# The dense stages of a decoder step in one block: the next stage begins on tiles 0 to 2 while tiles 3 and 4 are normalised

## The chip, the cores and the metric

The kernel runs on one core of a Trainium2 chip. The metric is the device time of one execution in microseconds (us); smaller is better. The core has five engines with a queue of their own: TensorE (PE), VectorE (DVE), ScalarE (ACT), GpSimd (POOL) and SyncE (SP), which here issues the loads. They meet through semaphores, and at the end of a block in a barrier of all engines.

## The reference

One step of a decoder of two layers, for 528 prompt tokens (16 of them learned) and 64 new tokens of 8 sequences, that is 592 tokens of width 1024. All is float32.

```
for l in range(DEPTH):                                    # DEPTH = 2, alpha = (2 * DEPTH) ** 0.25
    x = layernorm(alpha * x + 0.5 * swiglu(x, ffn1_w_in[l], ffn1_w_out[l]), ln1)
    z = x @ w_in[l]                                       # queries, keys, values, indexer, latents
    o = sparse_attention(z, cache_dsa) | latent_attention(z, cache_mla)
    x = layernorm(alpha * x + o @ w_o[l], ln2)
    x = layernorm(alpha * x + 0.5 * swiglu(x, ffn2_w_in[l], ffn2_w_out[l]), ln3)

def swiglu(x, w_in, w_out):                               # inner width 2816
    g, u = split(x @ w_in)
    return (silu(g) * u) @ w_out
```

## The kernel before

The 592 tokens are five tiles of rows: four of 128 and one of 80 (tile 4). `T.x` holds the residual, tokens on partitions. `T.xth` and `T.xtl` hold its transpose in two parts, a rounded high part and the remainder, so that a product in three passes (high x high, high x low, low x high) keeps float32's accuracy. Weights come in blocks of 128 x 1024 (512 KB) through a ring: SP loads one into one of four `raw` buffers, ACT rounds it into `whi` (`hi`, line 128), DVE subtracts into `wlo` (`lo`, line 132), both with two buffers, and PE uses it; `w_used` counts finished weights and frees the buffers.

The layer loop is a loop on the device (`Fori`). Its body is a row of blocks; each begins with branches and ends with a barrier that clears the block's semaphores: feed-forward 1 (`ffn_block`), projection (`proj_block`), index, prompt attention, two sample blocks, output projection (`mix_out_block`), feed-forward 2.

A feed-forward block first computes 44 products of width 592 (two matmuls of 296 columns for each of 8 slices and three passes, line 467, 48 per weight; the weight is the stationary operand); ACT takes silu, DVE multiplies, POOL splits the result into `hth` and `htl`. Then `out_stage` multiplies by the second weight, with the tokens stationary, in two groups: tiles 0 to 2 over all 22 slices, then tiles 3 and 4 (lines 140 to 142, 512 columns). While the second group runs, tiles 0 to 2 are normalised and transposed. `mix_out_block` uses the same `out_stage` with 8 slices and no first product.

The normalisation of a tile is a chain: DVE adds the product to alpha times x (`ln_sum`, 194) and takes the statistics (201, 203), ACT the root (211), DVE the reciprocal and the shift (217, 219), POOL scales and shifts, multiplies by the gain and adds the bias (227, 231, 233). For tiles 3 and 4 DVE does 640 of the 1024 columns (240, 244) and POOL the rest. Then PE transposes (260), ACT copies the high part (269), DVE subtracts the low part (274). For tiles 3 and 4 all this comes behind the last matmul, and the next block's first load is issued behind the barrier.

The projection multiplies by 14 weight parts: four column chunks of 338 in three slices of the inner dimension (`z_part`), and two parts of 384 columns for the latent queries (`q_part`). `Z_BANK` and `Q_BANK` say which PSUM bank each tile's result takes; small transposes (`job`) stand between the last parts, beginning with that of `wuk`. Every engine's order is that in which the code is written.

Of the kernel before, what the change touches and what calls it, by code (L numbers as in the profile page):

```python
# [88 lines left out]

class Map:  # L90
# [19 lines left out]
def stream_ops(T, S):  # L110
# [13 lines left out]
    def hi(e, n, s, round_, width=BLK, first=False):  # L124
        e.wait_ge(raw_in[s], round_ * 16 + 16)
        if not first:
            e.wait_ge(S.w_used, n - (SPLIT - 1))
        e.activation(T.whi[:, s % SPLIT, 0:width], T.raw[:, s, 0:width], ACT.Copy).then_inc(S.hi_done, 1)  # L128

    def lo(e, n, s, width=BLK):  # L130
        e.wait_ge(S.hi_done, n + 1)
        e.tensor_tensor(T.wlo[:, s % SPLIT, 0:width], T.raw[:, s, 0:width],  # L132
                        T.whi[:, s % SPLIT, 0:width].bitcast(F32), ALU.subtract).then_inc(S.split_done, 1)
# [14 lines left out]
TPB = {0: 2, 1: 4, 2: 2, 3: 4, 4: 2}  # L148


def out_stage(nc, T, S, kt, n0, lhs_hi, lhs_lo, scale, first_wait):
# [14 lines left out]
    rest = [t for t in GROUPS[0] if t not in turn.values()]  # L166

    def sp(e, weight, ln_g, ln_b, l):
        for g in range(2):
            for k in range(kt):  # L170
                n = n0 + g * kt + k
                load(e, n, n % RAW, weight(k), first=n < RAW)
                if g == 0 and k == kt // 2:
                    ln_wait = T.gb_free(S)
                    if ln_wait:
                        e.wait_ge(*ln_wait)
                    for i, a in enumerate((ln_g, ln_b)):
                        e.dma_start(T.gb[:, i, :], a[bass.ds(l, 1), :].partition_broadcast(P)).then_inc(S.gb_in, 16)
# [43 lines left out]
    def ln_d(e, t):  # L222
# [3 lines left out]
        e.wait_ge(S.nb_done, t + 1)  # L226
        e.tensor_scalar(x, x, T.rstd[0:r, t:t + 1], T.nb[0:r, t:t + 1], ALU.mult, ALU.add).then_inc(S.norm_done, 1)  # L227
# [5 lines left out]
        e.tensor_tensor(x, x, T.gb[0:r, 1, c], ALU.add).then_inc(S.x_done, 1)  # L233

# [12 lines left out]
    def ln_e(e, t):  # L247
# [5 lines left out]
        if t < 2:  # L253
            e.wait_ge(S.evac_done, 2 * (t + 1) + 2)
        else:
            e.wait_ge(S.xtl_done, t - 1)
        for k in range(KD):
            if t >= 3 and k == NV // P:
                e.wait_ge(S.x_done, t + 1)
            mm = e.transpose(T.ps[:, TPB[t] + k // 4, (k % 4) * P:(k % 4) * P + r],  # L260
# [3 lines left out]
    def tp(t):  # L264
        return T.ps[:, TPB[t]:TPB[t] + 2, :].rearrange("p b (q c) -> p (b q) c", q=4)[:, :, 0:ROWS[t]]
# [10 lines left out]
    def act(e):  # L276
        for g in range(2):
            for k in range(kt):
                n = n0 + g * kt + k + 2
                if n < n0 + 2 * kt:  # L280
                    act_split(e, n)
                if g == 1 and k in std_at:
                    ln_b(e, std_at[k])
                if g == 1 and k in turn:
# [4 lines left out]
        ln_b(e, 4)  # L289
        ln_f(e, 3)  # L290
        ln_f(e, 4)

    def dve(e):
        for g in range(2):
            for k in range(kt):
# [3 lines left out]
                if n < n0 + 2 * kt:  # L299
                    lo(e, n, n % RAW)  # L300
                if g == 1 and k > 0 and k in sum_at:
# [10 lines left out]
        for t in rest:  # L312
            ln_g(e, t)
        ln_dv(e, 3)
        ln_c(e, 4)
        ln_dv(e, 4)
# [7 lines left out]
    def pe(e):  # L324
# [24 lines left out]
        for t in [*rest, 3, 4]:  # L349
            ln_e(e, t)  # L350

    return sp, act, dve, pool, pe


FFN_SEMS = LN_SEMS + STREAM_SEMS + ["silu_done", "hmul_done", "hhi_done", "hlo_done"]


def ffn_block(nc, T, S, l, w_in, w_out, ln_g, ln_b):
# [4 lines left out]
    N1 = 2 * KF  # L363

# [5 lines left out]
    T.gb_free = lambda S_: (S_.hlo_done, KF)  # L370
    sp2, act2, dve2, pool2, pe2 = out_stage(nc, T, S, KF, N1, T.hth, T.htl, 0.5, first_wait)
# [4 lines left out]
    with nc.Block() as block:  # L376
        @block.sync
        def _(e):
            def four(i, first):
                for u in range(4):  # L380
                    j = 2 * i + u // 2
                    col = (u % 2) * D_FF + j * P
                    src = w_in[bass.ds(l, 1), :, bass.ds(col, P)].rearrange("l (k p) c -> p (l k) c", p=P)
                    load(e, 4 * i + u, u, src, shape=(KD, P), first=first)
            four(0, True)
            with e.Fori(1, KF // 2) as i:
                four(i, False)
            sp2(e, lambda k: w_out[bass.ds(l, 1), k * P:(k + 1) * P, :].rearrange("l p n -> p (l n)"), ln_g, ln_b, l)

        @block.scalar  # L390
        def _(e):
            def silu(i, u, first=False):
                e.wait_ge(S.w_used, 4 * i + 2 * u + 2)
                if not (first and u == 0):
                    e.wait_ge(S.hmul_done, 2 * i + u)
                e.activation(T.silu[:, :].rearrange("p (h c) -> p h c", h=2), bank(u, 0), ACT.Silu).then_inc(S.silu_done, 1)

            def body(i, first):
                for u in range(2):
# [2102 lines left out]
```

## Time and profile before

| | us |
|---|---|
| median of three runs | 3438.72 (3434.47 to 3439.16) |
| the profiled execution | 3437.44 |
| its span, first to last instruction | 3435.7 |
| PE busy | 3001.9 (87%) |
| weight loads of PE (beside it) | 2573.6 (75%) |
| DVE busy | 1428.0 (42%) |
| ACT busy | 999.6 (29%) |
| POOL busy | 624.9 (18%) |

The mean clock granted to TensorE was 0.933 of full speed. Busy times of matmuls overlap, since the next starts before the last has drained: the pace is the distance from start to start. A wait is shown with the engine, line and result that ended it. Names in the rows are those of the program, without buffer numbers.

### The profile page before, as it was taken

To read this page: it belongs to the slowest core of one execution; us is meant where nothing else is said; L and a number is where in the kernel's file an instruction comes from. 1 tells how busy PE (TensorE), PEld (TensorE's weight loads), DVE (VectorE), ACT (ScalarE), POOL (GpSimd) and SP (SyncE) were. 2 spreads that over 40 slices of the span, in tenths; PEclk is the share of its full clock that TensorE was granted. 3 is DMA by queue.
4 is the path that set the end of the run, shared out by engine and by line. 5 is a ranking of instruction groups with operands and counts; after the bars stand their busy time and mean duration, and the time that the engine had idled before them with its cause. 6 is when DMAs were issued, how large, how long until landed. Compare 5 with 4: busy or idle time off the path is not lost. (4 is left out here: it accounts for less than half of the span.)

```text
span 3435.7 us, 46122 instructions
## 1 busy us (share of the span) xinstructions
PE 3001.9 (87%) x18298; PEld 2573.6 (75%) x18298; DVE 1428.0 (42%) x2110; ACT 999.6 (29%) x1602; POOL 624.9 (18%) x568
## 2 busy tenths in 40 slices
PE   6999979768797879999889999796787978799997
PEld 6999759545565669998689997684555656699985
DVE  2222363466764352222622224434676643422236
ACT  2212233434342221212321223234344422212223
POOL 1111030213122131110311111211121121311103
PEclk9999989879898989999989999898798989899998
DMA  3222431300122322224432234313001223222244
GB/s 111 81 81 86 142 126 51 123 1 1 62 79 77 121 76 80 79 80 134 123 93 79 80 109 141 102 39 123 1 1 62 94 90 113 68 80 81 82 140 126
DMA packets 241752, 293.93 MB, mean 86 GB/s; under 512 B 12624, under 2 KB 205488, under 8 KB 235456
## 3 DMA queue, kind: packets, MB, share of 16 engines
q1 hardware_dynamic: 234688, 229.00, 22.2%
q0 software_dynamic: 6912, 62.92, 5.0%
q8 instruction: 94, 1.54, 0.2%
q14 instruction: 58, 0.48, 0.0%
HBM read 287.72 MB, written 3.88 MB: 85 GB/s over the span
## 5 line engine op out<-in xcount | busy, mean ns | idle before, releaser
L132 DVE TENSOR_TENSOR wlo<-raw,whi 128x1024 fp32r<-128x1024 f32 (+2 forms) x412 | 537.0, 1304 | 1430.5 <-ACT whi L128 1429.2
L128 ACT ACTIVATE whi<-raw 128x1024 fp32r<-128x1024 f32 (+2 forms) x412 | 433.5, 1052 | 1564.8 <-PE ps L467 928.4
L467 PE MATMUL ps<-xth,whi 128*128 128x296 f32 x2816 | 810.7, 300 | 42.3 <-DVE wlo L132 42.3
L467 PE MATMUL ps<-xtl,whi 128*128 128x296 f32 x2816 | 812.8, 301 | 0.0
L467 PE MATMUL ps<-xth,wlo 128*128 128x296 f32 x2816 | 615.6, 300 | 0.0
L467 PEld LDWEIGHTS ps<-xth,whi 128*128 128x128 f32 x2816 | 533.7, 190 | 43.2 <-DVE wlo L132 43.2
L467 PEld LDWEIGHTS ps<-xtl,whi 128*128 128x128 f32 x2816 | 532.2, 189 | 0.0
L467 PEld LDWEIGHTS ps<-xth,wlo 128*128 128x128 f32 x2816 | 460.7, 189 | 0.0
L140 PE MATMUL ps<-whi,hth 128*128 128x512 f32 (+1 forms) x880 | 350.7, 398 | 9.9 <-DVE wlo L132 8.3
L142 PE MATMUL ps<-whi,htl 128*128 128x512 f32 (+1 forms) x880 | 346.9, 394 | 0.0
L141 PE MATMUL ps<-wlo,hth 128*128 128x512 f32 (+1 forms) x880 | 346.8, 394 | 0.0
L446 POOL CAST hth<-hf 128x592 f32 x88 | 59.7, 678 | 989.0 <-DVE hf L417 989.0
L140 PE MATMUL ps<-whi,xth 128*128 128x338 f32 (+1 forms) x480 | 175.2, 365 | 43.4 <-DVE wlo L132 43.0
L140 PEld LDWEIGHTS ps<-whi,hth 128*128 128x128 f32 (+1 forms) x880 | 158.5, 180 | 67.7 <-DVE wlo L132 21.7
L142 PEld LDWEIGHTS ps<-whi,htl 128*128 128x128 f32 (+1 forms) x880 | 158.2, 180 | 45.9
L141 PEld LDWEIGHTS ps<-wlo,hth 128*128 128x128 f32 (+1 forms) x880 | 158.4, 180 | 42.1
L141 PE MATMUL ps<-wlo,xth 128*128 128x338 f32 (+1 forms) x480 | 170.0, 354 | 0.0
L142 PE MATMUL ps<-whi,xtl 128*128 128x338 f32 (+1 forms) x480 | 169.4, 353 | 0.0
L227 POOL TENSOR_SCALAR x<-x,rstd,nb 128x1024 f32<-128x1024 f32 (+2 forms) x30 | 34.7, 1158 | 652.7 <-DVE nb L219 652.7
L1599 ACT ACTIVATE pP<-ps,pnmx 128x256 f32<-128x256 f32 (+4 forms) x132 | 70.3, 532 | 232.9 <-DVE pnmx L1676 232.5
L140 PEld LDWEIGHTS ps<-whi,xth 128*128 128x128 f32 x480 | 91.5, 191 | 55.4 <-DVE wlo L132 46.1
L448 POOL TENSOR_TENSOR htl<-hf,hth 128x592 f32 x88 | 129.0, 1466 | 14.4 <-POOL hth L446 14.4
(378 smaller groups left out, 4014.8 us busy)
## 6 DMA issues: line engine op xcount, KB each, us to landing
raw<-in_ffn_w_in SPq DMA_DIRECT2D x176, 512.0 KB, 3.8
raw<-in_ffn_w_out SPq DMA_DIRECT2D x176, 512.0 KB, 3.5
raw<-in_w_o SPq DMA_DIRECT2D x32, 512.0 KB, 3.6
raw<-in_w_in SPq DMA_DIRECT2D x16, 507.0 KB, 3.7
gb<-in_ln_g SPq DMA_DIRECT2D x6, 512.0 KB, 4.6
gb<-in_ln_b SPq DMA_DIRECT2D x6, 512.0 KB, 6.0
raw<-in_w_in SPq DMA_DIRECT2D x8, 338.0 KB, 3.4
x<-in_x_prompt SPq DMA_DIRECT2D x1, 1536.0 KB, 10.8
```

The source lines that it names most:

```text
L128: e.activation(T.whi[:, s % SPLIT, 0:width], T.raw[:, s, 0:width], ACT.Copy).then_inc(S.hi_done, 1)
L132: e.tensor_tensor(T.wlo[:, s % SPLIT, 0:width], T.raw[:, s, 0:width], T.whi[:, s % SPLIT, 0:width].bitcast(F32), ALU.subtract).then_inc(S. ...
L140: e.matmul(out, lhi, rhi, start=start, stop=False)
L141: e.matmul(out, lhi, rlo, start=False, stop=False)
L142: return e.matmul(out, llo, rhi, start=False, stop=stop)
L227: e.tensor_scalar(x, x, T.rstd[0:r, t:t + 1], T.nb[0:r, t:t + 1], ALU.mult, ALU.add).then_inc(S.norm_done, 1)
L446: e.tensor_copy(h_hi, T.hf[:, u, :]).then_inc(S.hhi_done, 1)
L448: e.tensor_tensor(h_lo, T.hf[:, u, :], h_hi.bitcast(F32), ALU.subtract).then_inc(S.hlo_done, 1)
L467: mm = e.matmul(bank(u, up)[:, h, :], part[:, s, w], xp[:, k, o], start=(k == 0 and part is T.whi and xp is T.xth), stop=(k == KD - 1 and ...
L1599: e.activation(Pb[:, i % 3, 0:NK[t]], SB(p["s"], P, NK[t]), ACT.Exp, bias=nmx[:, i % 3:i % 3 + 1], accum_out=rsum[:, a, c:c + 1]).then_inc ...
```

## The change

The blocks of a run of dense stages become one block: feed-forward 1 and projection of layer 0; then output projection, feed-forward 2, feed-forward 1 of the next layer and its projection; at the end output projection and feed-forward 2. Five barriers with their semaphore clears fall away. The layer loop is written out in Python, since the last run of stages differs. Semaphores of the weight ring count on through a block (offset `B`), each stage has its own set for the rest.

- Weights of the next stage are loaded and split in the tail of the one before (`nxt.hi`, `nxt.lo`): two in the last two steps of the second group, two more between the steps of tiles 3 and 4. Up to four go to new buffers `awhi`, `awlo`, which lie over rows 0 to 13 of `hth`.
- A feed-forward stage that has one before it begins with four pieces on tiles 0 to 2 (384 columns), with the transposes of tiles 3 and 4 between them, and then four pieces on tiles 3 and 4 (208 columns). Its silu and product for these weights are made in two parts.
- The projection begins with its first six weight parts on tiles 0 to 2, the two transposes between, and then does the six on tiles 3 and 4.
- In the output projection the scale and shift of tiles 0 to 2 move from POOL to ACT (`ln_n`).
- Tile 3 and 4 are transposed into banks 6, 7 and 0, 1 (before a projection both into 0, 1); `Z_BANK`, `Q_BANK` and what the jobs wait for follow.
- Loads of the projection's gains, `wuk` and `wuv` are issued behind the load of its sixth part and behind the end of the normalisation. POOL scales x by alpha tile by tile behind the transposes.

```diff
@@ out_stage
+    act_norm = kt <= 12
@@ transposes, ln_e
-        else:
-            e.wait_ge(S.xtl_done, t - 1)
+        elif t == 2:
+            e.wait_ge(S.xtl_done, 1)
+        elif t == 3:
+            e.wait_ge(S.evac_done, 10 if tpb[0] == 0 else 8)
+        else:
+            e.wait_ge(S.evac_done, 10)
+            e.wait_ge(S.xtl_done, 4 if tpb[0] == tpb[1] else 1)
@@ ACT of out_stage
                 if n < n0 + 2 * kt:
                     act_split(e, n)
+                elif nxt:
+                    nxt.hi(e, n - n0 - 2 * kt)
                 if g == 1 and k in std_at:
                     ln_b(e, std_at[k])
+                if g == 1 and act_norm and k - 1 in std_at:
+                    ln_n(e, std_at[k - 1])
...
         ln_b(e, 4)
+        if nxt:
+            nxt.hi(e, 2)
+            nxt.hi(e, 3)
         ln_f(e, 3)
         ln_f(e, 4)
@@ DVE of out_stage
         for t in rest:
             ln_g(e, t)
+        if nxt:
+            nxt.lo(e, 2)
         ln_dv(e, 3)
         ln_c(e, 4)
+        if nxt:
+            nxt.lo(e, 3)
         ln_dv(e, 4)
@@ PE of a feed-forward stage
+        if early:
+            e.wait_ge(S0_.xtl_done, 3)
+            for u in range(2):
+                for up in range(2):
+                    cols, out = early_parts(u, up)[0]
+                    piece(2 * u + up, cols, out).then_inc(S.early_ps, 1)
+                    if up == 1 - u:
+                        stage.turn(e, 3 + u)
+            e.wait_ge(S0_.xtl_done, 5)
+            for u, up in ((1, 0), (0, 0), (0, 1), (1, 1)):
+                cols, out = early_parts(u, up)[1]
+                piece(2 * u + up, cols, out).then_inc(S.w_used, 1)
+        else:
             body(0, True)
@@ projection
-Z_BANK = [(0, 1, 2, 3, 4), (5, 6, 7, 0, 1), (2, 3, 4, 0, 1), (7, 3, 4, 5, 6)]
-Q_BANK = [(5, 6, 7, 2, 3), (4, 0, 1, 5, 6)]
+Z_BANK = [(2, 3, 4, 0, 1), (5, 6, 7, 2, 3), (4, 0, 1, 2, 3), (7, 4, 2, 3, 5)]
+Q_BANK = [(5, 6, 7, 4, 0), (1, 2, 3, 5, 6)]
...
                 elif b == 0:
-                    q_gone(e, 1, 1)
-                    q_gone(e, 1, 2)
+                    q_gone(e, 0, 4)
+                    q_gone(e, 1, 0)
...
-            for n in range(8):
-                z_part(n)
+            e.wait_ge(S0_.xtl_done, 3)
+            for n in range(3):
+                z_part(n, (0, 1, 2))
+            ln_e(e, 3)
+            e.wait_ge(S0_.evac_done, 8)
+            z_part(3, (0, 1, 2))
+            ln_e(e, 4)
+            z_part(4, (0, 1, 2))
+            z_part(5, (0, 1, 2))
+            e.wait_ge(S0_.xtl_done, 5)
+            for n in range(6):
+                z_part(n, (3, 4))
+            z_part(6)
+            z_part(7)
@@ build
-        with nc.Fori(0, DEPTH) as l:
-            ffn_block(nc, T, ffn_s, l, W["ffn1_w_in"], W["ffn1_w_out"], W["ln1_g"], W["ln1_b"])
-            proj_block(nc, T, proj_s, l, W, O)
+        dense_block(nc, T, dense_s, W, O, None, 0)
+        for l in range(DEPTH):
             index_block(nc, T, index_s, l, W["cache_dsa"])
             prompt_block(nc, T, prompt_s)
             sample_block(nc, T, sample_s, l, "M", W["cache_mla"], O["mla_s"], W["cache_dsa"])
             sample_block(nc, T, sample_s, l, "D", W["cache_dsa"], O["dsa_s"])
-            mix_out_block(nc, T, ffn_s, l, W["w_o"], W["ln2_g"], W["ln2_b"])
-            ffn_block(nc, T, ffn_s, l, W["ffn2_w_in"], W["ffn2_w_out"], W["ln3_g"], W["ln3_b"])
+            dense_block(nc, T, dense_s, W, O, l, l + 1 if l + 1 < DEPTH else None)
```

TensorE, from the output projection into feed-forward 2, before: the last matmuls on tile 4, the transposes of tiles 2 to 4 (`ident`, `x`), the branches of block end and begin, the first product.

```order
L142 MATMUL ps<-whi_53,xtl_51 80x512
L260 MATMUL ps<-ident_58,x_49 128x128 x16
L260 MATMUL ps<-ident_58,x_49 128x80 x8
L2417 UNCONDITIONAL_BRANCH
L451 UNCONDITIONAL_BRANCH
L467 MATMUL ps<-xth_50,whi_53 128x296
```

TensorE at the same place now (`awhi` and `awlo` are the weights split ahead):

```order
L168 MATMUL ps<-whi_53,xtl_51 80x512
L300 MATMUL ps<-ident_58,x_49 128x128 x8
L580 MATMUL ps<-xth_50,awhi_83 128x384
...
L580 MATMUL ps<-xth_50,awlo_84 128x384
L300 MATMUL ps<-ident_58,x_49 128x128 x8
L580 MATMUL ps<-xth_50,whi_53 128x384
...
L580 MATMUL ps<-xth_50,wlo_54 128x384
L300 MATMUL ps<-ident_58,x_49 128x80 x8
L580 MATMUL ps<-xth_50,whi_53 128x384
...
L580 MATMUL ps<-xth_50,wlo_54 128x384
L580 MATMUL ps<-xth_50,whi_53 128x208
```

The transposes of tile 3 stand behind 48 matmuls of 384 columns, those of tile 4 behind 24 more, and the width of 208 follows behind 24 more again.

VectorE, at the end of feed-forward 1 and the beginning of the projection, before:

```order
L203 BN_AGGR mv<-stats 80x2
L240 SCALAR_TENSOR_TENSOR x<-x,mv,gb 128x640
L244 SCALAR_TENSOR_TENSOR x<-x,rstd,gb 128x640
L217 RECIPROCAL rstd<-std 80x1
...
L244 SCALAR_TENSOR_TENSOR x<-x,rstd,gb 80x640
L274 TENSOR_TENSOR xtl<-ps,xth 128x8x128
L274 TENSOR_TENSOR xtl<-ps,xth 128x8x80
L376 UNCONDITIONAL_BRANCH
L997 UNCONDITIONAL_BRANCH
L1055 MEMSET z 64x1352
L1056 MEMSET qpe 64x256
L132 TENSOR_TENSOR wlo<-raw,whi 128x1014 x2
```

VectorE at the same place now:

```order
L232 BN_AGGR mv<-stats 80x2
L159 TENSOR_TENSOR awlo<-raw,awhi 128x676
L275 SCALAR_TENSOR_TENSOR x<-x,mv,gb 128x640
L279 SCALAR_TENSOR_TENSOR x<-x,rstd,gb 128x640
L246 RECIPROCAL rstd<-std 80x1
L248 SCALAR_TENSOR_TENSOR nb<-mv,rstd 80x1
L159 TENSOR_TENSOR awlo<-raw,awhi 128x1014
L275 SCALAR_TENSOR_TENSOR x<-x,mv,gb 80x640
L279 SCALAR_TENSOR_TENSOR x<-x,rstd,gb 80x640
L314 TENSOR_TENSOR xtl<-ps,xth 128x8x128
L314 TENSOR_TENSOR xtl<-ps,xth 128x8x80
L1228 MEMSET z 64x1352
```

A weight split (`awlo`) stands ahead of each of tiles 3's and 4's normalised columns; the memsets of `z` and `qpe` still stand behind the last subtraction, in front of the fifth weight's split.

ScalarE at the same place before, from the last weight copy of the feed-forward stage:

```order
L128 ACTIVATE whi<-raw 128x1024
L211 ACTIVATE std<-mv,eps 128x1
L211 ACTIVATE std<-mv,eps 80x1
L269 ACTIVATE xth<-ps 128x8x128
L269 ACTIVATE xth<-ps 128x8x80
L376 UNCONDITIONAL_BRANCH
L929 UNCONDITIONAL_BRANCH
L128 ACTIVATE whi<-raw 128x1014 x2
L128 ACTIVATE whi<-raw 128x676
```

ScalarE now:

```order
L153 ACTIVATE whi<-raw 128x1024
L153 ACTIVATE awhi<-raw 128x1014 x2
L240 ACTIVATE std<-mv,eps 128x1
L240 ACTIVATE std<-mv,eps 80x1
L153 ACTIVATE awhi<-raw 128x676
L153 ACTIVATE awhi<-raw 128x1014
L309 ACTIVATE xth<-ps 128x8x128
L309 ACTIVATE xth<-ps 128x8x80
L153 ACTIVATE whi<-raw 128x1014
L153 ACTIVATE whi<-raw 128x676
```

Four weight copies have moved ahead of the copies of tiles 3 and 4 (`xth`); the fifth, of the second slice of chunk 1, stands behind both.

## Rows read from the trace of the kernel before

**Rows 1.** Page, parts 1 and 2: busy time, slices of TensorE.
```profile
PE 3001.9 (87%) x18298; PEld 2573.6 (75%) x18298; DVE 1428.0 (42%) x2110; ACT 999.6 (29%) x1602; POOL 624.9 (18%) x568
...
PE   6999979768797879999889999796787978799997
```

**Rows 2.** Waits of PE, whole span: us in total, times, longest us.
```profile
PE ps L140 <- DVE wlo L132: 54.8, 18, 13.6
...
PE ps L467 <- DVE wlo L132: 42.3, 4, 12.4
```

**Rows 3.** Stretches: us, busy of PE PEld DVE ACT POOL, PEclk, DMA, GB/s.
```profile
484.40:508.60 24.20, 3.56 (x16) 2.68 (x16) 12.94 (x21) 4.26 (x6) 7.65 (x9) 0.56 0.31 100
1708.80:1732.80 24.00, 3.56 (x16) 2.68 (x16) 11.53 (x19) 4.65 (x6) 11.52 (x11) 0.58 0.23 63
1236.30:1257.00 20.70, 3.56 (x16) 2.68 (x16) 11.76 (x19) 5.11 (x7) 11.53 (x11) 0.63 0.28 74
```

**Rows 4.** Timeline, feed-forward to projection, layer 0: start, us, engine, line [idle <-releaser].
```profile
483.99 0.40 PE L142 MATMUL ps<-whi,htl 128*80 128x512 f32 x1
...
490.19 0.89 DVE L244 SCALAR_TENSOR_TENSOR x<-x,rstd,gb 128x640 f32<-128x640 f32 x1
...
492.23 1.10 DVE L244 SCALAR_TENSOR_TENSOR x<-x,rstd,gb 80x640 f32<-80x640 f32 x1
...
494.27 0.99 POOL L233 TENSOR_TENSOR x<-x,gb 80x384 f32<-80x384 f32 x1
...
501.76 8.77 SPq L122 DMA_DIRECT2D raw<-in_w_in  x6
...
506.27 1.05 ACT L128 ACTIVATE whi<-raw 128x1014 fp32r<-128x1014 f32 x1 [9.55 <-DMA raw<-in_w_in]
...
508.62 0.65 PE L140 MATMUL ps<-whi,xth 128*128 128x338 f32 x1 [12.64 <-DVE wlo L132]
```

**Rows 5.** Chain that ended last, in order of time: start, us, what.
```profile
2960.18 291.81 PE ps L467 x2112
...
3378.57 0.87 PE ps L260 x8
```

**Rows 6.** Timeline of PE, first latent product: first and last of 24 intervals.
```profile
571.00 0.33 PE L141 MATMUL ps<-wlo,cqh 128*128 128x384 f32 x1
...
575.19 0.33 PE L141 MATMUL ps<-wlo,cqh 128*80 128x384 f32 x1
```

**Rows 7.** Stretches of PE: us, PE busy (instructions), PEclk, DMA share, GB/s.
```profile
508.60:515.00 6.40, 6.38 (x24) 0.53 0.60 171
518.60:525.60 7.00, 7.00 (x47) 1.00 0.28 74
1226.40:1229.40 3.00, 2.95 (x11) 0.50 0.00 0
1272.70:1708.80 436.10, 433.64 (x2701) 1.00 0.33 100
```

**Rows 8.** Timeline of ACT: the weight copies that end the compared stretches.
```profile
548.92 1.05 ACT L128 ACTIVATE whi<-raw 128x1014 fp32r<-128x1014 f32 x1 [3.59 <-PE ps L142]
...
1285.95 1.06 ACT L128 ACTIVATE whi<-raw 128x1024 fp32r<-128x1024 f32 x1 [5.51 <-PE ps L467]
...
1761.13 1.06 ACT L128 ACTIVATE whi<-raw 128x1024 fp32r<-128x1024 f32 x1 [5.51 <-PE ps L467]
```

**Rows 9.** Timeline: two waits of PE, two instructions of DVE.
```profile
586.59 1.11 PE L1163 MATMUL ps<-ident,wuk 128*128 128x128 f32 x4 [3.87 <-DVE qpe L1053]
...
1215.81 3.24 DVE L132 TENSOR_TENSOR wlo<-raw,whi 128x1024 fp32r<-128x1024 f32 x1
...
1226.45 1.97 PE L260 MATMUL ps<-ident,x 128*128 128x128 f32 x8 [4.30 <-POOL x L233]
...
1240.04 1.17 DVE L274 TENSOR_TENSOR xtl<-ps,xth 128x1024 fp32r<-128x1024 f32 x1
```

**Rows 10.** Page, part 5: the weight splits; busy us, mean ns | idle.
```profile
L132 DVE TENSOR_TENSOR wlo<-raw,whi 128x1024 fp32r<-128x1024 f32 (+2 forms) x412 | 537.0, 1304 | 1430.5 <-ACT whi L128 1429.2
```

More of the change, by code:

```diff
@@ new lines, in weight_lo, with sync, four @@
+    def weight_lo(e, n):
+        lo(e, B + n, n % RAW, ahead=AHEAD.get(n))
+    stage.nxt = Ahead(weight_hi, weight_lo)
+    def sync(e):
+        def four(i, first):
+            for u in range(4):
+                j = 2 * i + u // 2
+                col = (u % 2) * D_FF + j * P
+                src = w_in[bass.ds(l, 1), :, bass.ds(col, P)].rearrange("l (k p) c -> p (l k) c", p=P)
+                load(e, B + 4 * i + u, u, src, shape=(KD, P), first=first)
+        four(0, B == 0)
+        with e.Fori(1, KF // 2) as i:
+            four(i, False)
+        stage.sp2(e, lambda k: w_out[bass.ds(l, 1), k * P:(k + 1) * P, :].rearrange("l p n -> p (l n)"), ln_g, ln_b, l)
@@ new lines, in tensor, with piece, body @@
+    def tensor(e):
+        def piece(n, cols, out):
+            w_hi = T.awhi[:, AHEAD[n], :] if n in AHEAD else T.whi[:, n % SPLIT, :]
+            w_lo = T.awlo[:, AHEAD[n], :] if n in AHEAD else T.wlo[:, n % SPLIT, :]
+            e.wait_ge(S.split_done, B + n + 1)
+            for k in range(KD):
+                w = slice(k * P, (k + 1) * P)
+                for part, xs in ((w_hi, (T.xth, T.xtl)), (w_lo, (T.xth,))):
+                    for xp in xs:
+                        mm = e.matmul(out, part[:, w], xp[:, k, cols], start=(k == 0 and part is w_hi and xp is T.xth),
+                                      stop=(k == KD - 1 and part is w_lo))
+            return mm
+        def body(i, first):
+            for u in range(2):
+                for up in range(2):
+                    n = 4 * i + 2 * u + up
+                    s = up % SPLIT
+                    e.wait_ge(S.split_done, B + n + 1)
+                    if up == 0 and not first:
+                        e.wait_ge(S.hmul_done, 2 * i + u - 1)
+                    for k in range(KD):
+                        w = slice(k * P, (k + 1) * P)
+                        for part, xs in ((T.whi, (T.xth, T.xtl)), (T.wlo, (T.xth,))):
+                            for h in range(2):
+                                o = slice(h * HALF, (h + 1) * HALF)
+                                for xp in xs:
+                                    mm = e.matmul(bank(u, up)[:, h, :], part[:, s, w], xp[:, k, o],
+                                                  start=(k == 0 and part is T.whi and xp is T.xth),
+                                                  stop=(k == KD - 1 and part is T.wlo))
+                    mm.then_inc(S.w_used, 1)
+        if early:
+            e.wait_ge(S0_.xtl_done, 3)
+            for u in range(2):
+                for up in range(2):
+                    cols, out = early_parts(u, up)[0]
[6 more added lines that the diff above has]
+                piece(2 * u + up, cols, out).then_inc(S.w_used, 1)
+        else:
+            body(0, True)
+        with e.Fori(1, KF // 2) as i:
+            body(i, False)
+        stage.pe2(e)
+        if stage.last:
+            stage.ln_e(e, 3)
+            stage.ln_e(e, 4)
@@ L478, with begin, end @@
+    def begin(ln_e):
+        stage.turn = ln_e
+    def end(nxt, tpb=(6, 0)):
+        stage.sp2, stage.act2, stage.dve2, stage.pool2, stage.pe2, stage.ln_e = \
+            out_stage(nc, T, S, KF, B + N1, T.hth, T.htl, 0.5, first_wait, nxt, tpb, gb_free=(S.hlo_done, KF))
+        stage.last = nxt is None
+    stage.begin, stage.end = begin, end
+    stage.parts = (sync, scalar, vector, gpsimd, tensor)
+    return stage
 C_ROPE = 0
```

449 lines of the change are left out of this document (264 added, 185 removed).

## The prediction

> **What bounds the kernel now.** The page's first part has TensorE busy 87% of the span and every other engine under half [rows 1]: time is won where TensorE stands still or is slow. The waits of TensorE say where. Its two costliest kinds of wait on a weight split (`wlo`, line 132) are few and long: 54.8 us in 18 waits, the longest 13.6, and 42.3 us in only 4 [rows 2]. Waits that long sit at the stage boundaries. The table of stretches shows three kinds of them: 24.2 us behind the first feed-forward stage, 24.0 between the two layers, 20.7 behind an output projection, each with 3.6 us of TensorE work, the transposes [rows 3]. The five that the change touches (two of the first kind, one, two) are some 114 us, 3.3% of the span.
>
> The order of time in the first one [rows 4]: the last matmul ends at 484.4; VectorE finishes tile 3's normalised columns at 491.1 and tile 4's at 493.3, GpSimd tile 4's at 495.3; then the barrier; only at 501.8 is the first weight load issued, ScalarE splits it at 506.3, TensorE starts at 508.6. And it starts slowly: for 6.4 us the granted clock is 0.53, the lower level, about 3 us lost [rows 7].
>
> **Pace of TensorE.** 296 columns: 291.81 us for 2112 matmuls, 0.138 us each, 0.137 without the slow start. 384 columns: 24 matmuls in 4.19 us (571.00 to 575.19), 0.175. 338 columns: 7.00 us for a chunk's 45, 0.156. Eight transposes of 128 columns: 0.87, 0.109 each [rows 5 to 7]. The change makes a width that the trace lacks, 208 columns: not under the transposes' 0.109, not over 0.137 of the 296 columns; the line through 296 and 384 would give 0.10. I take 0.11, near the lower row. The four early weights then cost 96 x (0.175 + 0.11) = 27.4 us instead of 192 x 0.137 = 26.3: 1.1 us more per stage, up to 3.7.
>
> The Trainium skill, TensorE: Matmul & The Clock Gate, section LDWEIGHTS, gives a 128-column weight load 128/1.2 = 107 ns, which would be a floor for the narrow pieces. The transposes' 109 ns agrees, so by the rule too they cost 0.11.
>
> **Between the layers (one boundary).** Counted from the end of the last matmul, t = 0. The first two weights are split ahead, into space that the second product has left, while its last steps run: ScalarE and VectorE are mostly idle there. Pieces (0,0) and (0,1) on 384 columns end at 8.4. The transposes of tile 3 want its normalised columns. Before, these were there at 6.7 (491.1 less 484.4). Now the split of weight 2 stands ahead of them on VectorE: it waits for ScalarE, which copies only behind tile 4's root (some 1.4), and takes 1.3 itself (mean 1304 ns) [rows 4, 10]; 0.4 more come from the splits ahead of tile 3's sums. So 9.7, a wait of 1.3. Then 0.9 transposes, 4.2 piece, tile 4 (ready at about 14.1: 10.9 before, plus a second split and the delay, less what GpSimd does beside it; reached at 14.8), 0.8, 4.2, and four narrow pieces 10.6: 30.4 us for four weights. Before, ScalarE took the sixth weight at 1761.1, when TensorE had done with four: 52.3 us after 1708.8 [rows 3, 8]. Gain 21.9. What runs beside it on ScalarE (silu in two parts) and on GpSimd (the scaling by alpha, tile by tile behind the transposes) has 6.6 us of matmuls per weight to hide in.
>
> **Feed-forward to projection (two).** Three weights on tiles 0 to 2: 72 x 0.156 = 11.2; transposes 0.9; fourth weight 4.2; transposes of tile 4 0.7: t = 17.0. The next weight is not ready. Its copy stands on ScalarE behind the copy of tile 4 (0.7), and on VectorE the subtraction of tile 4 (0.8), two memsets (1.5) and the split (1.2) come one after another: 21.4, so 4.4 us idle. Then 45 + 96 matmuls, 22.0, and 0.8 for weight 6, whose buffer comes free only 12 matmuls before it is wanted: 44.2. An idle time of this length is answered by the lower clock: behind 4.30 us of idle the three microseconds from 1226.4 ran at 0.50, 1.5 lost, and a little more behind them [rows 7, 9]. I put 2 us: 46.2. Before, the same point was at 548.9, 64.5 us after the last matmul [rows 8]. Gain 18.3 each, 36.6.
>
> **Output projection to feed-forward (two).** Here tile 2 is transposed last, and its low part is subtracted on VectorE behind the sums of tiles 3 and 4: at 1240.04 for 1.17 [rows 9]. The first early piece waits for it: TensorE stands still from 1236.3 to about 1240.7, and pays 2 us of lower clock. Then 8.4 + 0.9 + 4.2 + 0.8 + 4.2 + 10.6 = 29.1: 1271.8, against 1285.9 before [rows 8]. Gain 14.1 each, 28.3. Inside this stage the first affine step of tiles 0 to 2 moves from GpSimd to ScalarE. Tile 0 gets later by about 0.5 us (it stands behind a weight copy), tile 1 earlier by about 1, so the 4.30 us wait at 1226.45 shrinks a little; tile 2 stands behind the copy of tile 1's transposes and a weight copy. I take nothing; it can be 3 either way.
>
> **Inside the projection (two).** New PSUM banks: the transposes of `wuk` waited 3.87 us for a `qpe` copy of VectorE [rows 9]; now they want only copies that ScalarE makes first, and the VectorE copy is wanted by tile 2, one tile later. Some 1 us of wait stays; with the clock 3.5 us each, 7.0 (bounds 0 and 11).
>
> **Things costed at nothing.** The layer loop is written out. Code entered for the first time shows no cost: TensorE's slices read alike, within a tenth or two, in the loop's first pass (the first 20) and its second [rows 1]. The parameter loads move behind the weights of the projection and behind the end of the normalisation, about 30 us before they are wanted.
>
> **Sum.** 21.9 + 36.6 + 28.3 + 7.0 = 93.8. The profiled execution took 3437.4 (span 3435.7), 1.3 under the median: 3438.7 - 94 = 3344.7. I predict 3344.
>
> A rule that speaks against it: the Trainium skill, GPSIMD Engine Reference, Specifications, says that GpSimd shares its SBUF interfaces with VectorE, and that instructions of VectorE with two SBUF inputs contend. The weight split is one, and the change puts two of them into the tail where GpSimd normalises. The trace agrees that a split can take 3.24 us [rows 9]. By the rule the tail is up to 3.9 us longer per boundary; this is the first rival.
>
> **Rivals.**
> 1. The tail grows. Splits beside GpSimd take 3.24 instead of 1.30 us [rows 9, 10]: two per boundary, 3.9 us, five times: 19 us, and some more half clock, about 3368. For it: tile 4's work on GpSimd falls beside the second split. Against: between the sums and that, GpSimd has finished tile 3, and TensorE has 8 to 17 us of pieces in hand.
> 2. Narrow matmuls are slow. If one of 208 columns costs as two passes of 0.11, 288 of them cost 32 us more: 3376. Nothing in the trace has that width; the 8 transposes at 0.109 speak against it.
> 3. The waits that I see are shorter and the clock stays up: five waits of 4 us with 2 us each would give back up to 18: 3326.
> 4. The pieces start no earlier: their weights wait for rows of the second product or for raw buffers. Only the barrier and the load (12 us per boundary) would be saved at most, perhaps half: about 3400.
> 5. Slower. Without its pauses TensorE is granted the lower clock for long. The place is the feed-forward stage behind each boundary, 292 us of its first product. A quarter of that work at half speed adds 73 us, three times 219: 3563. It decides from 188 us at half clock, whose half eats the gain. Against: 1272.7 to 1708.8 ran without a pause at 1.00 [rows 7]; every fall follows idle time.
>
> **How the numbers follow.** The forecast 0.62, rival 1 0.17, rival 2 0.06, rival 3 0.09, rival 4 0.03, rival 5 0.03. The range: downwards rival 3 (3326). Upwards the bounds together: narrow pieces at 0.137 (+8), tail 2 us longer each (+10), nothing from the banks (+7), clock 3 instead of 2 (+4): 3373; to take in rival 2, 3376. About 0.9 would lie inside by the cases; I leave it, since several of these terms are unseen. A change under 0.2% (7 us) could not be told from none: faster 0.96, within 0.01, slower 0.03.
>
> **What would show it.** TensorE's waits on `wlo` fall from about 100 to about 45 us. Between the layers TensorE has no gap over 2 us. Behind each feed-forward stage there is one gap of 4 to 5 us in front of the fifth projection weight, behind each output projection one of about 4.5 in front of the first 384-column matmul. The 208-column matmuls start 0.11 us apart. The granted clock dips below 1 only behind those gaps; its mean rises from 0.933 to about 0.94. It is wrong if a gap over 6 us stays at any of the five, or if the half clock lasts over 5 us behind one.

## The result and the profile after

The changed kernel takes 3344.0 us (median of 4 runs, 3343.0 to 3345.8), the kernel before 3438.1 on the same chip: a ratio of 0.9729, 95% interval 0.9712 to 0.9746. The forecast was 3344. The profiled execution took 3345.84 us, with a span of 3343.8 against 3435.7, and a mean granted clock of 0.946 against 0.933.

Page, part 1 and TensorE's slices, as in [rows 1]:

```profile
PE 2992.7 (90%) x18298; PEld 2567.1 (77%) x18298; DVE 1424.6 (43%) x2116; ACT 1002.0 (30%) x1612; POOL 623.7 (19%) x562
...
PE   6999998768797889999999999986888968899997
```

TensorE is busy for 9 us less than before, in a span 92 us shorter. The dips of the slices to 7 at the stage boundaries are gone, but for an 8 at the end of each output projection; what is left is attention. The waits of PE (us in total, times, longest us); L166 was L140, L598 was L467, L159 was L132 [rows 2]:

```profile
PE ps L166 <- DVE wlo L159: 37.9, 20, 8.4
...
PE ps L300 <- POOL x L263: 16.9, 7, 3.6
...
PE ps L598 <- DVE wlo L159: 11.9, 1, 11.9
...
PE ps L580 <- DVE xtl L314: 6.5, 2, 3.6
...
PE ps L166 <- DVE qpe L1225: 1.9, 2, 0.9
```

97.1 us on weight splits have become 49.8, and 11.9 of these are the kernel's first weight, which nothing can precede. Stretches of the kernel after (us, busy of PE PEld DVE ACT POOL, PEclk, DMA share, GB/s), to be held against [rows 3, 7, 8]:

```profile
484.77:506.60 21.83, 17.14 (x117) 16.90 (x115) 15.41 (x26) 5.51 (x8) 8.72 (x9) 1.00 0.32 106
506.60:510.20 3.60, 3.60 (x13) 3.60 (x14) 0.72 (x1) 0.00 (x0) 0.00 (x0) 0.53 0.97 309
510.20:531.20 21.00, 20.33 (x130) 19.41 (x128) 1.63 (x3) 2.18 (x4) 0.00 (x0) 1.00 0.02 6
1145.43:1249.94 104.51, 92.78 (x472) 78.33 (x473) 53.03 (x66) 32.81 (x37) 30.90 (x20) 0.94 0.38 121
1672.80:1703.12 30.32, 29.28 (x209) 28.91 (x208) 14.84 (x24) 7.29 (x10) 13.84 (x13) 1.00 0.31 89
```

The fourth row is the first output projection up to the fourth early weight. The last row is the boundary between the layers: four weights in 30.3 us, TensorE busy for 29.3 of them, full clock. Behind a feed-forward stage (first three rows) the one pause ends at 506.60, and the clock is 0.53, the lower of its two levels, for 3.6 us behind it. The timeline shows what that pause is made of:

```profile
502.68 0.82 DVE L314 TENSOR_TENSOR xtl<-ps,xth 128x640 fp32r<-128x640 f32 x1 [3.19 <-ACT xth L309]
503.84 1.19 DVE L1228 MEMSET z<- 64x1352 f32 x1 [0.34 <-issue]
505.03 0.27 DVE L1229 MEMSET qpe<- 64x256 f32 x1
505.33 1.99 DVE L159 TENSOR_TENSOR wlo<-raw,whi 128x1014 fp32r<-128x1014 f32 x2
...
506.60 0.61 PE L166 MATMUL ps<-whi,xth 128*128 128x338 f32 x1 [4.69 <-DVE wlo L159]
```

VectorE is idle for 3.19 us, then has tile 4, two memsets and the split in a row. ScalarE's copy of that weight ended at 503.6, before the memsets began. The same in the other projection (4.70).

**Where the 92 us are.** Each stretch is taken between the same points of both traces: it begins with the end of the feed-forward stage's last matmul or with the start of the output projection's first one, and ends where ScalarE begins the weight copy that waits for the last of these weights, as in [rows 8] (up to 0.3 us behind the end of the matmuls, where the rows above end).

| stretch | before | after | gain | forecast |
|---|---|---|---|---|
| end of feed-forward to six projection weights done, layer 0 / 1 | 64.5 / 65.2 | 46.1 / 46.5 | 18.4 / 18.7 | 18.3 / 18.3 |
| first output projection to four weights done | 118.9 | 104.8 | 14.2 | 14.1 |
| second output projection, the same | 119.2 | 106.3 | 12.8 | 14.1 |
| between the layers, four weights | 52.3 | 30.4 | 21.9 | 21.9 |
| projection, latent product to attention, layer 0 / 1 | 56.8 / 58.2 | 53.8 / 53.9 | 2.9 / 4.4 | 3.5 / 3.5 |

The sum is 93.3, the spans differ by 91.9; the rest of the program is 1.4 us longer (the first stage by 1.4, the attention stages -1.9 and +1.8, which is less than their scatter, see layers_written_out). In the five boundary stretches, 86.1 us shorter, TensorE's busy time fell from 310.7 to 299.6 us: 75 us are time that it no longer stands still, 11 are matmuls that no longer run at the lower clock.

### The profile page after: what moved, and what is told of

It is laid out like the page before. It is cut to its first block and busy times, and to the rows that moved or that the text cites. A ratio compares the mean times of both kernels' runs of the same rounds, so it can differ in the third digit from the quotient of the medians.

```text
span 3343.8 us, 45553 instructions
## 1 busy us (share of the span) xinstructions
PE 2992.7 (90%) x18298; PEld 2567.1 (77%) x18298; DVE 1424.6 (43%) x2116; ACT 1002.0 (30%) x1612; POOL 623.7 (19%) x562
## 5 line engine op out<-in xcount | busy, mean ns | idle before, releaser
L159 DVE TENSOR_TENSOR wlo<-raw,whi 128x1024 fp32r<-128x1024 f32 (+2 forms) x398 | 512.0, 1288 | 1295.3 <-ACT whi L153 1294.2
L598 PE MATMUL ps<-xth,whi 128*128 128x296 f32 x2624 | 752.7, 299 | 11.9 <-DVE wlo L159 11.9
L598 PE MATMUL ps<-xtl,whi 128*128 128x296 f32 x2624 | 755.2, 300 | 0.0
L598 PE MATMUL ps<-xth,wlo 128*128 128x296 f32 x2624 | 572.3, 300 | 0.0
L598 PEld LDWEIGHTS ps<-xth,whi 128*128 128x128 f32 x2624 | 495.2, 189 | 12.0 <-DVE wlo L159 12.0
L598 PEld LDWEIGHTS ps<-xtl,whi 128*128 128x128 f32 x2624 | 493.9, 188 | 0.0
L598 PEld LDWEIGHTS ps<-xth,wlo 128*128 128x128 f32 x2624 | 428.0, 189 | 0.0
L166 PE MATMUL ps<-whi,hth 128*128 128x512 f32 (+1 forms) x880 | 350.6, 398 | 10.0 <-DVE wlo L159 8.3
L166 PEld LDWEIGHTS ps<-whi,hth 128*128 128x128 f32 (+1 forms) x880 | 158.5, 180 | 67.8 <-DVE wlo L159 22.5
L166 PE MATMUL ps<-whi,xth 128*128 128x338 f32 (+3 forms) x370 | 137.3, 371 | 28.3 <-DVE wlo L159 26.2
L167 PE MATMUL ps<-wlo,xth 128*128 128x338 f32 (+3 forms) x370 | 132.7, 359 | 0.0
L168 PE MATMUL ps<-whi,xtl 128*128 128x338 f32 (+3 forms) x370 | 132.3, 358 | 0.0
L1724 PE MATMUL ps<-z,pPT 128*128 128x128 f32 (+1 forms) x672 | 105.1, 292 | 22.6 <-DVE posb L1888 22.6
## 6 DMA issues: line engine op xcount, KB each, us to landing
x<-in_x_prompt SPq DMA_DIRECT2D x1, 1536.0 KB, 10.4
```

The costliest lines, as they stand in the source:

```text
L159: e.tensor_tensor(w_lo, T.raw[:, s, 0:width], w_hi.bitcast(F32), ALU.subtract).then_inc(S.split_done, 1)
L166: e.matmul(out, lhi, rhi, start=start, stop=False)
L167: e.matmul(out, lhi, rlo, start=False, stop=False)
L168: return e.matmul(out, llo, rhi, start=False, stop=stop)
L598: mm = e.matmul(bank(u, up)[:, h, :], part[:, s, w], xp[:, k, o], start=(k == 0 and part is T.whi and xp is T.xth), stop=(k == KD - 1 and ...
L1724: mm = e.matmul(flat[:, o:o + w], PT[0:kr, u % 2, k * P:(k + 1) * P], v, start=k == kts[0][0], stop=k == kts[-1][0])
```

## The experiments

Each was timed in five rounds (no_overlap in three) beside the kernel before, in three batches, each on another chip. The changed kernel was not timed again with them, so variants of it are compared with it by their ratios to the kernel before; a ratio of 0.001 is 3.4 us, and two such ratios are each known to about 0.0015.

### banks_alone

```
-Z_BANK = [(0,1,2,3,4), (5,6,7,0,1), (2,3,4,0,1), (7,3,4,5,6)]
-Q_BANK = [(5,6,7,2,3), (4,0,1,5,6)]
+Z_BANK = [(2,3,4,0,1), (5,6,7,2,3), (4,0,1,2,3), (7,4,2,3,5)]
+Q_BANK = [(5,6,7,4,0), (1,2,3,5,6)]     # and their waits
```

> The kernel before with nothing changed but the PSUM banks of the projection and the waits that follow from them. The theory of the prediction: 3.5 us less in each of two projections, so 3438.1 - 7 = 3431 us; in the profile the 3.87 us wait of the wuk transposes for a qpe copy shrinks to about 1 us. Rival: the copies of the other engine are as late, and the wait only changes its name and place: 3438 us, the sum of TensorE's waits inside the projection unchanged.

3431.8 us, ratio 0.9979 (0.9970 to 0.9989): 7.2 us less. The wait of [rows 9] is gone from the `wuk` transposes and one of 0.94 stands a tile later; timeline of PE in banks_alone:

```profile
588.15 0.42 PE L140 MATMUL ps<-whi,xth 128*128 128x338 f32 x1 [0.94 <-DVE qpe L1053]
```

From the latent product to attention it is 53.5 us instead of 56.8. The rival (the wait only changes its name) is out.

### no_overlap

```
 e.wait_ge(S0_.xtl_done, 3)
+stage.turn(e, 3); stage.turn(e, 4)      # transposes of tiles 3 and 4
+e.wait_ge(S0_.xtl_done, 5)
 ... pieces, without transposes between; the projection alike
```

> The changed kernel with TensorE's order put back at all five boundaries: tiles 3 and 4 are transposed and split first, and only then come the first weights' matmuls, on all tiles. One block, no barrier, and the weights loaded and split ahead as in the changed kernel. By my reasons the overlap is worth 13 us between the layers (four weights done 44 us after the last matmul, not 30.4), 10 at each of the two boundaries to the projection and 6 at each of the two behind an output projection: 45 us, and with five pauses of 10 to 16 us some 3 us more, so 3344 + 48 = 3392 us. If the barrier and the weight load were the whole gain: 3344 to 3350. If the overlap were all of it: about 3430.

3406.2 us, ratio 0.9907 (0.9891 to 0.9922): of the 94 us only 32 are left, so the overlap of the tail with matmuls is worth 62, two thirds. Of the 32 some 7 belong to the new PSUM banks (banks_alone), which this kernel has too. What is left for the barriers that are gone, the weights that are loaded and split early, the loop written out and the shifted affine step is about 25 us by the times, 30 by the traces of the five boundaries (420.1 to 389.8 us), a quarter to a third. No run takes these apart. TensorE's timeline in no_overlap, behind the first feed-forward stage and between the layers:

```profile
492.72 1.94 PE L300 MATMUL ps<-ident,x 128*128 128x128 f32 x8 [8.87 <-DVE x L279]
497.13 1.36 PE L300 MATMUL ps<-ident,x 80*128 80x80 f32 x8 [2.47 <-DVE xtl L314]
500.14 0.65 PE L166 MATMUL ps<-awhi,xth 128*128 128x338 f32 x1 [1.65 <-DVE xtl L314]
...
1705.01 1.94 PE L300 MATMUL ps<-ident,x 128*128 128x128 f32 x8 [9.53 <-DVE x L279]
```

And the stretch that answers to the 30.3 us:

```profile
1695.32:1741.46 46.14, 32.72 (x210) 31.71 (x209) 14.81 (x24) 7.28 (x10) 13.72 (x13) 0.82 0.20 58
```

The last piece ends 46.1 us after the last matmul, forecast 44: the pauses are answered by a mean clock of 0.82, where the changed kernel has 1.00 at this boundary. Over the five boundaries the traces show 56 us lost (389.8 instead of 334.1), forecast 48. TensorE's busy time there is 313.1 instead of 299.6 us, so the lower clock took 13.5 us, where I had put 3; standing still took 42, where I had put 45. The timed runs lost 62; 6 of these I cannot place. The profiled execution (span 3398) was the fastest of the four.

### layers_written_out and banks_and_written_out

```
-        with nc.Fori(0, DEPTH) as l:
+        for l in range(DEPTH):
```

> The kernel before with the loop over the layers written out, no other edit. The prediction costed this at nothing: 3438 us, within 2. Rival: code entered for the first time has to be fetched and the second layer is slower by more than it was: some 5 to 20 us longer, with gaps of all engines at the stage starts of the second layer. Other rival: constant addresses in place of registers shorten the start of every stage: 3430 us.

3432.5 us, ratio 0.9977 (0.9968 to 0.9986): 7.9 us less for an edit that I had costed at nothing. The second rival came near in the time (3430), but not in its mechanism: the start of the projection of layer 0 is no shorter (13.70 us of wait for its first weight, 12.64 before). To see whether that stands, the loop was written out on top of banks_alone:

> The kernel before with the new PSUM banks of the projection and with the layer loop written out. The two together, if layers_written_out measured something that stands: 3438.5 x 0.9979 x 0.9977 = 3423 us. If its 8 us were chance: 3431 us, as banks_alone. In the profile I look at the stretch between the layers, where the first weight's wait was 12.43 us with the loop and 9.84 without: about 9.8 again if it belongs to the loop's end, 12.3 to 13.7 as at the other boundaries if not.

3423.0 us, ratio 0.9945 (0.9932 to 0.9959): it stands. The first feed-forward matmul of the second layer, at 1732.81 behind 12.43 us of wait in the kernel before, in layers_written_out and in banks_and_written_out:

```profile
1734.19 0.61 PE L467 MATMUL ps<-xth,whi 128*128 128x296 f32 x1 [9.84 <-DVE wlo L132]
```

```profile
1727.13 0.62 PE L467 MATMUL ps<-xth,whi 128*128 128x296 f32 x1 [9.12 <-DVE wlo L132]
```

So the loop's end costs 2.6 us (12.43 to 9.84) to 4.6 (13.70 in banks_alone to 9.12). The wait for the first projection weight of layer 1 is 12.33 us in both, instead of 13.62 and 13.01, but the same wait in layer 0, which the edit does not touch, lies anywhere between 12.64 and 13.70 in these four traces, so that difference shows nothing. The other 3 to 5 of the 8 us stay open. The attention stages, where they could be, scatter too much to tell: that of layer 0 takes 537.5 to 545.8 us in kernels that have the same code for it. In the changed kernel the 2.6 to 4.6 us are part of the waits that the overlap removes, and so cannot be had twice.

### no_scalar_affine

```
-    act_norm = kt <= 12
+    act_norm = False
```

> The changed kernel with the affine step of tiles 0 to 2 of the output projection back on GpSimd. The prediction costed this edit at nothing, with 3 us per stage either way. Having seen the profile after, I expect 3345 us, within 2: the transposes of tile 2 may start a microsecond earlier or later, but the first early piece waits for VectorE, which takes tile 2's low part only behind the sums of tiles 3 and 4 (1217.32). Rival: GpSimd is the bound of the stage, and one more pass over three tiles (1.2 to 2.1 us each) shows at full price: 3344 + 2 x 4 = 3352 us.

3350.9 us, ratio 0.9745 (0.9732 to 0.9758), 5 to 7 us over the changed kernel. The intervals of the two ratios overlap, but the traces show a loss too: the fourth early weight is done 3.3 us later in the first of the two stages and 1.8 in the second. My 3345 was wrong and the rival nearer. In the first output projection, VectorE, GpSimd and TensorE in no_scalar_affine:

```profile
1209.72 1.97 PE L300 MATMUL ps<-ident,x 128*128 128x128 f32 x8 [4.30 <-POOL x L263]
...
1213.92 5.30 DVE L159 TENSOR_TENSOR awlo<-raw,awhi 128x1024 fp32r<-128x1024 f32 x2
1219.14 1.28 DVE L223 SCALAR_TENSOR_TENSOR x<-ps,x 128x512 f32<-128x512 f32 x2
...
1214.88 3.25 POOL L263 TENSOR_TENSOR x<-x,gb 128x1024 f32<-128x1024 f32 x1
...
1226.34 0.69 PE L580 MATMUL ps<-xth,awhi 128*128 128x384 f32 x1 [7.06 <-DVE xtl L314]
```

And in the changed kernel:

```profile
1203.54 1.09 PE L300 MATMUL ps<-ident,x 128*128 128x128 f32 x8 [2.35 <-POOL x L263]
...
1206.87 1.22 DVE L159 TENSOR_TENSOR awlo<-raw,awhi 128x1024 fp32r<-128x1024 f32 x1
1208.75 2.67 DVE L159 TENSOR_TENSOR awlo<-raw,awhi 128x1024 fp32r<-128x1024 f32 x1 [0.66 <-ACT awhi L153]
1211.34 1.27 DVE L223 SCALAR_TENSOR_TENSOR x<-ps,x 128x512 f32<-128x512 f32 x2
...
1217.32 1.17 DVE L314 TENSOR_TENSOR xtl<-ps,xth 128x1024 fp32r<-128x1024 f32 x1
...
1213.68 1.97 PE L300 MATMUL ps<-ident,x 128*128 128x128 f32 x8 [3.56 <-POOL x L263]
...
1218.54 0.69 PE L580 MATMUL ps<-xth,awhi 128*128 128x384 f32 x1 [2.89 <-DVE xtl L314]
```

The first piece starts 77.2 us into the stage, against 73.1 (77.2 and 74.2 in the second stage). The transposes of tile 2 are not the reason: they come at 69.0 and 69.1 us, against 68.2 and 69.3. The reason is VectorE's order. Tile 2's low part stands behind the sums of tiles 3 and 4, these behind the two splits ahead, and the splits behind tile 1's low part. With the affine step on GpSimd tile 1 is transposed at 60.5 us instead of 58.1 (59.2 in the second stage), and the splits begin at 64.7 instead of 61.4 (62.5): 3.3 and 2.3 us. Only 0.8 us more come from the splits themselves, which take 5.2 us from the start of the first to the end of the second instead of 4.5, both beside GpSimd instead of one. So the rival's reason holds in part: the pass on GpSimd stands in the chain of tile 1. The edit that I took as neutral is worth about 2 to 3 us per stage.

### fifth_weight_ahead

```
 nxt.hi(e, 3)
+if nxt.more: nxt.hi(e, 4)     # ScalarE, before ln_f(3)
 ...
 ln_dv(e, 4)
+if nxt.more: nxt.lo(e, 4)     # VectorE, before ln_g(3)
 ...                           # memsets behind weight_lo(5)
```

> The changed kernel with the fifth projection weight split ahead as well: its copy stands on ScalarE ahead of the copies of tiles 3 and 4, its subtraction on VectorE behind tile 4's affine step, and the two memsets behind the subtraction of the sixth weight. My theory: the 4.69 and 0.60 us waits in front of the projection's fifth and sixth weights go, and with the first of them the twelve matmuls at 0.287 in place of 0.156 us (1.6 us): 6.9 us in each of two projections, so 3344 - 14 = 3330 us. Rival: the wait only moves, to the sixth weight, whose split now stands behind tile 4's subtraction, or to tiles 3 and 4: under 2 us each, 3341 us.

3332.1 us, ratio 0.9685 (0.9672 to 0.9698): 12 us (medians) to 15 (ratios) under the changed kernel, 14 forecast. The split falls into the idle time of VectorE seen above, and the fifth weight follows the transposes of tile 4 without a wait (VectorE, then TensorE, in fifth_weight_ahead):

```profile
496.46 1.20 DVE L159 TENSOR_TENSOR wlo<-raw,whi 128x1014 fp32r<-128x1014 f32 x1
...
500.58 0.72 PE L300 MATMUL ps<-ident,x 80*128 80x80 f32 x8
501.10 0.40 PE L166 MATMUL ps<-whi,xth 128*128 128x338 f32 x1
```

The 0.60 us stay. They stand in front of weight 6, whose buffer comes free only 12 matmuls before it is wanted, and I had put them into the gain wrongly.

### tile2_shared, order_alone, tile2_shared_first

Two edits, apart and together: the affine step of tile 2 on VectorE and GpSimd by columns, and tile 2's low part ahead of the sums of tiles 3 and 4.

```
+    dv0 = 2 if act_norm else 3     # first tile that is shared by columns
-        ln_a(e, 3); ln_c(e, 3); ln_a(e, 4); ln_g(e, 2)
+        ln_g(e, 2); ln_a(e, 3); ln_c(e, 3); ln_a(e, 4)
```

> The changed kernel with tile 2 of the output projection normalised as tiles 3 and 4 are: 640 columns on VectorE, 384 on GpSimd, no affine step on ScalarE. In the profile after, TensorE waits 3.56 us for tile 2's normalised columns (1213.68), then 2.89 for its low part (1218.54). My theory is that VectorE's queue sets the first early piece, since the low part of tile 2 stands behind the sums of tiles 3 and 4: the transposes come 3.5 us earlier and nearly all of it goes into a longer wait for the low part; what is left is some 1.3 us, because a split ahead no longer shares its time with GpSimd: 3344 - 2 x 1.3 = 3341 us. Rival: the chain from the mean of tile 2 to its transposes sets it, and the 3.5 us come back in full at both boundaries, with the clock: 3335 us.

> The changed kernel, and ScalarE copies and VectorE subtracts tile 2's transposes ahead of the sums of tiles 3 and 4, while tile 2 is normalised as in the changed kernel (by ScalarE and GpSimd). By my theory each half of the pair is worth nothing by itself: the transposes of tile 2 still come at 1213.7, so its low part is ready only 0.6 us earlier, and the sums of tiles 3 and 4 start some 6 us later, which the 9 us of early pieces just cover: 3344 us, between 3342 and 3348. Rival: the order was the whole of the gain of tile2_shared_first: 3333 us.

> The same as tile2_shared, and ScalarE copies and VectorE subtracts tile 2's transposes ahead of the sums of tiles 3 and 4. If VectorE's queue was what was left, the first early piece comes 5.1 us earlier than in the changed kernel (1213.4 in its times), TensorE stands 2.3 us instead of 3.56 and 2.89, and about 2 us of half clock go; tile 3 is wanted when it is just ready, 0.3 to 1 us of wait. 6.5 us at each of two boundaries: 3331 us. Rival: tiles 3 and 4 get later by the 2 us by which their sums are pushed back, and TensorE waits there for what it won: 3340 us.

Sharing alone: 3346.8 us, ratio 0.9731 (0.9718 to 0.9744), no gain, where I had expected 3341. Order alone: 3342.3, 0.9723 (0.9709 to 0.9736), within the error of the changed kernel. Both: 3332.6, 0.9684 (0.9671 to 0.9698), 11 to 15 us. In the traces the two stages up to their fourth early weight are shorter by 0.5, 2.6 and 10.4 us together. The first early piece in tile2_shared and in tile2_shared_first:

```profile
1225.33 0.69 PE L583 MATMUL ps<-xth,awhi 128*128 128x384 f32 x1 [5.71 <-DVE xtl L315]
```

```profile
1218.76 0.44 PE L587 MATMUL ps<-xth,awhi 128*128 128x384 f32 x1 [2.37 <-DVE xtl L315]
```

With sharing alone 3.56 and 2.89 us of wait became one of 5.71 (8.73 in the second output projection), and the piece starts 72.8 us into the stage; with both, 69.3, and 69.0 in the second, against 73.1 and 74.2 in the changed kernel. Two chains of about one length end in that piece, and shortening either by itself shows the other.

### all_three

Both edits above, and between the layers the third weight's subtraction behind tile 3's affine step.

> The edits of fifth_weight_ahead and tile2_shared_first together, and in front of a feed-forward stage the third weight's subtraction behind tile 3's affine step on VectorE, which takes the 1.04 us wait between the layers. They stand at different boundaries, so they should add up: 3344 - 14 - 13 - 1 = 3316 us. Rival: TensorE without its pauses is granted less in the stages behind, and the sum falls short by more than 5 us.

3317.5 us, ratio 0.9646 (0.9633 to 0.9660), where 3316 was expected: the gains add up, and the clock (0.950) does not answer with a loss. The 1.04 us in front of tile 3's transposes between the layers are gone; the two output projections with their four weights take 100.2 and 99.7 us instead of 104.8 and 106.3.

## Why the prediction was right

The time came out as forecast to a microsecond, and the stretches one by one to within 1.3 us. The last microsecond is luck: the profiled executions differ by more than that in stages that no edit touches, and one stretch came right by terms that cancel (below).

**Between the layers.** Each step came as put down. Timeline between the layers of the kernel after:

```profile
1679.39 1.22 DVE L159 TENSOR_TENSOR wlo<-raw,whi 128x1024 fp32r<-128x1024 f32 x1 [1.31 <-ACT whi L153]
1680.53 0.88 DVE L275 SCALAR_TENSOR_TENSOR x<-x,mv,gb 128x640 f32<-128x640 f32 x1
1681.53 0.88 DVE L279 SCALAR_TENSOR_TENSOR x<-x,rstd,gb 128x640 f32<-128x640 f32 x1
...
1682.47 1.09 PE L300 MATMUL ps<-ident,x 128*128 128x128 f32 x8 [1.04 <-DVE x L279]
1687.61 0.72 PE L300 MATMUL ps<-ident,x 80*128 80x80 f32 x8
1692.42 0.26 PE L580 MATMUL ps<-xth,whi 128*128 128x208 f32 x1
1692.51 0.28 PE L580 MATMUL ps<-xtl,whi 128*128 128x208 f32 x1
1692.62 0.28 PE L580 MATMUL ps<-xth,wlo 128*128 128x208 f32 x1
1692.74 0.27 PE L580 MATMUL ps<-xth,whi 128*128 128x208 f32 x1
```

The split of weight 2 does stand ahead of tile 3's columns (wait 1.04, forecast 1.3), tile 4 is not waited for, and 208 columns go at 0.111 us (0.11). That excludes rival 2. The Trainium skill (TensorE: Matmul & The Clock Gate, LDWEIGHTS) gives P / 1.2 ns for a load of P columns, by estimate 107 ns for 128; the 0.111 us at 208 columns and the 0.109 of the transposes at 128 agree with such a floor.

**Feed-forward to projection.** One wait of 4.69 (4.4 forecast) and 1.6 us of half clock (2), a gain of 18.4 and 18.7. The 0.8 for weight 6 was put at the wrong place: its 0.60 stand just behind the stretch, and within it TensorE waits 0.63 for a copy of `z`. fifth_weight_ahead shows that the wait was the order of the instructions, and not the weight's load or tile 4. It moved the copy on ScalarE and the split on VectorE together; that VectorE's queue was the later of the two is read from the trace (the copy ended at 503.6, the split began at 505.33).

**Output projection to feed-forward.** The sum was right to 1.3 us (14.2 and 12.8 for 14.1), by errors that cancel. The term "inside this stage nothing, 3 either way" was right in size only. I had let tile 2's transposes start when they did before, 68.2 and 68.4 us into the stage, and they start at 68.2 and 69.3. But the last matmul of the stage ends 3.7 and 2.8 us earlier than before, since TensorE waits 5.2 and 3.6 us in front of the transposes of tiles 0 and 1 instead of 6.0, and in the first of the two stages loses 2.9 us less to the lower clock. It then stands for 3.56 us in front of tile 2's, which I had not seen: tile 2's affine step waits on ScalarE, as I wrote, "behind the copy of tile 1's transposes and a weight copy", and its two steps on GpSimd take 2.50 and 3.21 us beside the splits ahead (2.37 and 2.40 before). The second pause, for tile 2's low part, was 2.89 and 3.62 us instead of 4.4; the lower clock cost 3.2 and 2.9 instead of 2. (By [rows 9] the subtraction of the low part ends at 1241.2 before, half a microsecond later than I took it.) The second output projection, from the transposes of tile 2 on, and the stretch that ran at the lower clock (us, PE busy, PEclk, DMA share, GB/s):

```profile
2861.06 1.24 PE L300 MATMUL ps<-ident,x 128*128 128x128 f32 x8 [3.56 <-POOL x L263]
2865.93 0.69 PE L580 MATMUL ps<-xth,awhi 128*128 128x384 f32 x1 [3.62 <-DVE xtl L314]
```

```profile
2865.93:2872.00 6.07, 6.07 (x19) 0.50 0.30 89
```

**The signs put down beforehand.** The waits on `wlo` (49.8 us for about 45), the mean clock (0.946 for 0.94), the one gap behind feed-forward (4.69, 4.70), the largest between the layers (1.04) and the pace of 208 columns came. Two did not: at each output projection there were two gaps, not one, and behind the later of the two the half clock lasted 4.96 us in the first output projection and 6.1 in the second, over the 5 us that I had named as a sign of being wrong. What had failed there is the account of tile 2's wait, not the sum.

**Inside the projection.** 2.9 and 4.4 in the traces, 7.2 us for two in banks_alone: the 7.0 put down.

**The loop at nothing.** Wrong by itself (8 us), harmless in the sum: 2.6 to 4.6 us of it lie in a wait that was counted with the boundary between the layers, and the rest is not placed. Had the change written the loop out and kept the barriers, I would have said "same" to a kernel that is 0.23% faster.

**The rivals.** Rival 1 did not grow the tail at the boundaries behind feed-forward stages: the splits between the tiles took 0.86, 1.20 and 1.22 us, and GpSimd's first step on tile 4, 2.20 us beside the second split instead of 1.23, was covered by the pieces. It lives in the output projection. The Trainium skill (GPSIMD Engine Reference, Specifications) names the shared SBUF interfaces; the 5.30 us for two splits beside GpSimd (alone about 2.4) agree with that. Rival 3 had shorter waits and no half clock behind them; waits of 4.7 us with 1.6 us of lower clock were there. Rival 4 is what no_overlap makes: 30 us at five boundaries in its trace, 6 each, half of the 12 as rival 4 had it, and so the smaller part of the gain. Rival 5: behind the boundaries the clock stayed at its upper level, as in the feed-forward stage behind the first output projection:

```profile
1250.00:1672.00 422.00, 419.54 (x2602) 382.76 (x2602) 136.46 (x131) 106.31 (x114) 68.28 (x52) 1.00 0.33 105
```

## What to carry to other kernels

Where a stage ends in a tail of vector work, begin the next stage on the tiles that are finished: here that was worth two thirds of the gain, while the barriers and the early weights together were worth a quarter to a third. Then read what stands in each queue between the last tile and the first weight: a memset or a split that nobody wants yet costs TensorE its full time and, behind it, some microseconds of lower clock. If two chains end in the same instruction, change both before you judge either.

## What was not expected of the hardware

- A pause of 4.69 us cost 1.6 us more in clock behind it (0.53 for 3.6 us); pauses of 3.56 and 2.89 us close together cost about 3 (matmuls of 384 columns at 0.32 instead of 0.175 us, and transposes at 0.21 instead of 0.109). Pauses of this length should be priced at a third to a half above their length; one of 1.04 us was followed by full clock. The same pause of 3.56 us was followed by transposes at half pace in the first output projection and at full pace (0.11 us) in the second.
- VectorE's weight split and a GpSimd instruction did not run side by side. In the kernel before 37 splits took over 1.5 us instead of 1.2; each of them ended 1.06 to 1.09 us after the end of a GpSimd instruction, and so did all 34 in the changed kernel (1.06 to 1.10). The price of a split is thus what is left of the GpSimd instruction that it meets: 2.67 us (1208.75) beside one that ended at 1210.34. It works the other way too: GpSimd's next step took 3.21 us instead of 2.4.
- A loop over the two layers on the device cost 8 us against the same code written out, of which 2.6 to 4.6 are seen at the loop's edge.
